# A two-layer decoder trunk with routed experts: the router's product taken ahead of the norm, the first expert weights asked for later, and the operand splits in another order

## The reference, cut to what matters

```python
for i in range(DEPTH):                       # DEPTH = 2, SEQ = 512, D_MODEL = 1024
    mix = swa_sink_attention(...) if i % 2 == 0 else forgetting_attention(...)
    x = layer_norm(ALPHA * x + mix, ln_gain[i, 0], ln_bias[i, 0])
    ffn = grouped_moe(x, w_router, b_router, w_gate[i], w_up[i], w_down[i])
    x = layer_norm(ALPHA * x + ffn, ln_gain[i, 1], ln_bias[i, 1])

def layer_norm(x, gain, bias):
    mu, var = mean(x), mean((x - mu) ** 2)
    return (x - mu) * rsqrt(var + 1e-5) * gain + bias

def grouped_moe(h, ...):                     # 16 experts in 4 groups of 4
    logits = h @ w_router + b_router         # (512, 16)
    # softmax; the best group by its two highest scores; in it the best two experts
    # act = silu(h @ w_gate[e]) * (h @ w_up[e]) * gate;  y = sum over e of act @ w_down[e]
```

## Time and profile before

| | |
|---|---|
| median of 3 runs | 919.23 us (918.41 to 920.52) |
| the profiled execution's own time | 919.96 us |
| its span | 918.2 us |
| TensorE busy | 888.0 us (97%) |
| VectorE busy | 552.9 us (60%) |
| ScalarE busy | 392.3 us (43%) |
| granted TensorE clock, mean | 0.996 |

### The profile page before, as it was taken

The page is one execution under the profiler, slowest core; times in us unless marked ns, Lnnn a source line. Parts: engine busy times, 40 slices in busy tenths (PEclk is TensorE's granted clock), DMA queues, the critical chain, the costliest instruction groups (busy, mean ns, idle before and its releaser), DMA issues.

```text
span 918.2 us, 12501 instructions
## 1 busy us (share of the span) xinstructions
PE 888.0 (97%) x4480; PEld 616.2 (67%) x4480; DVE 552.9 (60%) x1141; ACT 392.3 (43%) x787; POOL 120.1 (13%) x138
## 2 busy tenths in 40 slices
PE   8999999999999999989999999999999999999996
PEld 7887777884666665557878886655786565666553
DVE  4544786548766677773332223777456777677846
ACT  4322787001555655540132224777301355555540
POOL 2000232103010000120000000323111200000030
PEclk9999999999999999999999999999999999999999
DMA  9962000019999998644054222120106999999352
GB/s 347 302 253 92 2 1 1 24 47 351 350 382 389 379 389 322 222 180 163 21 184 138 92 93 92 46 71 24 69 24 241 312 380 382 374 384 406 124 197 96
DMA packets 49446, 182.36 MB, mean 199 GB/s; under 512 B 6496, under 2 KB 6496, under 8 KB 41200
## 3 DMA queue, kind: packets, MB, share of 16 engines
q1 hardware_dynamic: 35712, 132.34, 38.6%
q0 software_dynamic: 9392, 34.12, 11.3%
q10 hardware_dynamic: 4288, 15.21, 4.2%
HBM read 159.60 MB, written 22.05 MB: 198 GB/s over the span
## 4 chain that ended last, share of the span: by engine, by line
PE 89%; DVE 5%; DMA 3%; issue 2%; ACT 1%; SPq 1%; POOL 0%; DVEq 0%; ACTq 0%; POOLq 0%
PE bank L613 17%; PE bank L615 16%; PE bank L614 16%; PE bank L896 11%; PE bank L727 4%; PE bank L708 4%; PE bank L865 3%; PE bank L570 3%; PE bank L752 2%; PE bank L771 2%; PE bank L527 2%; DMA ring<-in_swa_w_in 2%; PE bank L813 2%; PE bank L541 1%; DMA ys<-arena 1%
## 5 line engine op out<-in xcount | busy, mean ns | idle before, releaser
L1492 DVE TENSOR_TENSOR gu_low<-ring,gu_high 128x1024 fp32r<-128x1024 f32 x128 | 151.2, 1221 | 46.9 <-ACT gu_high L1116 46.8
L1116 ACT CAST gu_high<-ring 128x1024 fp32r<-128x1024 f32 x128 | 127.6, 1048 | 18.5 <-DVE arena L1626 18.5
L896 PE MATMUL bank<-ring,arena 128*96 128x512 f32 x256 | 115.8, 595 | 2.0 <-issue 2.0
L613 PE MATMUL bank<-gu_high,rows_high 128*96 128x512 f32 x256 | 113.0, 442 | 2.5 <-DVE rows_low L1610 2.5
L614 PE MATMUL bank<-gu_low,rows_high 128*96 128x512 f32 x256 | 101.5, 397 | 0.0
L615 PE MATMUL bank<-gu_high,rows_low 128*96 128x512 f32 x256 | 101.1, 395 | 0.0
L896 PEld LDWEIGHTS bank<-ring,arena 128*96 128x96 f32 x256 | 39.7, 164 | 55.0 <-issue 54.0
L1048 ACT ACTIVATE arena<-arena,nmax 128x256 f32<-128x256 f32 (+3 forms) x128 | 66.8, 523 | 20.9 <-DVE nmax L1385 10.8
L471 POOL TENSOR_TENSOR low<-ring,high 128x512 fp32r<-128x512 f32 x32 | 40.7, 1272 | 220.5 <-ACT high L1076 220.5
L613 PE MATMUL bank<-high,x_high 128*128 128x512 f32 x160 | 64.2, 401 | 1.3 <-DVE low L1286 1.1
L615 PE MATMUL bank<-high,xlow 128*128 128x512 f32 x160 | 62.9, 393 | 0.0
(11 more groups left out here) (244 smaller groups left out, 1543.7 us busy)
## 6 DMA issues: line engine op xcount, KB each, us to landing
ring<-in_w_gate SPq DMA_DIRECT2D x32, 1024.0 KB, 12.3
ring<-in_w_up SPq DMA_DIRECT2D x32, 1024.0 KB, 15.0
ring<-in_w_down SPq DMA_DIRECT2D x32, 1024.0 KB, 14.9
ring<-in_fox_w_in SPq DMA_DIRECT2D x6, 2048.0 KB, 9.4
ys<-arena ACTq DMA_DIRECT2D x28, 384.0 KB, 7.7
ys<-lnp POOLq DMA_DIRECT2D x1, 4608.0 KB, 24.3
ring<-in_swa_w_in SPq DMA_DIRECT2D x2, 2048.0 KB, 17.2
ring<-in_swa_w_o SPq DMA_DIRECT2D x2, 2048.0 KB, 15.9
```

Source lines behind the costliest of these rows:

```text
L613: eng.matmul(out, ah, wh, start=(c == 0), stop=False)
L896: mm = eng.matmul(bank[5 + half][0:CAP, :], hT[:, b, c, :], w[:, c, half * BLK:(half + 1) * BLK], start=(c == 0), stop=(c == FC - 1))
L1116: eng.copy(gu_high[u % 2][:, :, part, :], slot_gate_up(use)[:, :, part, :]).then_inc(S("gu_high"), 1)
L1492: eng.tensor_tensor(gu_low[use % RING][:, :, part, :], slot_gate_up(use)[:, :, part, :], gu_high[u % 2][:, :, part, :], ALU.subtract).then ...
```

## The change

Four edits. First, the router's product is taken of the residual before the norm. With r the reciprocal root and mu the mean of a row, logits = r * (x @ (gain*wr - mean over rows of gain*wr)) + (bias @ wr + br). The adjusted weights and biases of both layers are made once, in the last four groups of layer 0's projection: four more small loads, a transpose and a product on PE, some twelve small operations on DVE. `turn_x` waits for `res_done` and no longer for `x_ready`; DVE copies the transposed tile first and applies the norm then (`turned_norm`); the routing has one more operation of 64 elements (rows times r).

Second, the third tile's router product stands inside the last group of the output projection, and the 16 dummy matmuls behind it are 3.

Third, SP asks for less before the routing. `down 0` is still asked for at the end of the output projection; gate and up 2, down 1, gate and up 3 and down 2 wait for the first expert's rows, down 3 for the second's.

Fourth, orders: expert 0's low parts are made in pairs at t = 1 and t = 2; six of the eight value-weight subtractions ahead of the mixed statistics go behind the first tile's norm; the banks are opened ahead of the hot rows' transposes; the rope load shares a semaphore with tile 1's load.

```diff
@@ SP
+                        for i in range(2 * DEPTH):
+                            vec = (ln_gain, ln_bias)[i % 2][i // 2, 0]
+                            eng.dma_start(ln_rows[KC * i:KC * i + KC, :], vec.rearrange("(c p) -> c p", p=P)).then_inc(S("const_in"), 16)
...
                 eng.wait_ge(S(f"wo_done{l}"), OUT_BLOCKS * NT)
-                for u in range(RING):
+                load_down(EXP_USE[l], l, 0, S(f"d_loaded{EXP_USE[l] % RING}"))
+                for u in range(1, RING):
+                    if u < RING - 1:
+                        eng.wait_ge(S(f"xe_in{l}0"), 16)
+                    else:
+                        eng.wait_ge(S(f"xe_in{l}1"), 16)
+                    if u + 1 < RING:
+                        k = EXP_USE[l] + u + 1
+                        load_gate_up(k, l, u + 1, S(f"w_loaded{k % RING}"))
                     k = EXP_USE[l] + u
-                    if u == RING - 1:
-                        eng.wait_ge(S(f"xe_in{l}1"), 16)
-                    if u >= OUT_BLOCKS:
-                        load_gate_up(k, l, u, S(f"w_loaded{k % RING}"))
                     load_down(k, l, u, S(f"d_loaded{k % RING}"))
@@ PE
+                elif a in ("00", "10"):
+                    eng.wait_ge(S("res_done"), 2 * (t + 1) + OUT_BLOCKS * NT * int(a[0]))
...
+                            if k == GROUPS[0] - 4:
+                                eng.wait_ge(S("const_in"), 144)
+                                eng.transpose(bank[7][:, 0:4 * KC], ln_rows[0:4 * KC, :], ident[0:4 * KC, 0:4 * KC]).then_inc(S("wr_pe"), 1)
+                            if k == GROUPS[0] - 3:
+                                eng.wait_ge(S("consts"), 1)
+                                eng.wait_ge(S("wr_dve"), 1)
+                                eng.matmul(bank[7][:, 0:4 * NE], ones, wr_sum, start=True, stop=True).then_inc(S("wr_pe"), 1)
+                    eng.wait_ge(S("wr_dve"), 2)
...
+                            if g == OUT_BLOCKS * NT - 1 and c == KC // 2:
+                                route(t - 1)
...
-                    if t >= 1:
+                    if 1 <= t < NT - 1:
                         route(t - 1)
-                hum(16)
+                hum(3)
                 turn_x(NT - 1, f"{l}0")
@@ ACT
                 for t in range(NT):
+                    evac_x(f"{l}0", t)
                     eng.wait_ge(S(f"x_ready{l}0"), t + 1)
                     eng.dma_start(xd[t * P:(t + 1) * P, :], xres[:, t, :]).then_inc(S("x_stored"), 16)
-                    evac_x(f"{l}0", t)
@@ DVE
+                def turned_norm(t):
+
+                    v = xres[:, t, :]
+                    evac_x_tile(f"{l}0", t)
...
+                    link(eng.scalar_tensor_tensor(v, v, mv[:, t, 0:1], lnp[:, 0, :], ALU.subtract, ALU.mult))
+                    eng.wait_ge(S(f"rstd{l}0"), t + 1)
+                    eng.scalar_tensor_tensor(v, v, rstd[:, t:t + 1], lnp[:, 1, :], ALU.mult, ALU.add).then_inc(S(f"x_ready{l}0"), 1)
...
-                link(eng.tensor_tensor(lg, lps, tiles(br[:, :]), ALU.add))
+                link(eng.tensor_tensor(lg, lps, over(rstd[:, :], NE), ALU.mult))
+                link(eng.tensor_tensor(lg, lg, tiles(bl[:, l, :]), ALU.add))
...
-                    value_weights_low(KC, 2 * KC)
+                    value_weights_low(KC, KC + 2)
...
                                 state_low(t - 1)
+                                if t == 1:
+                                    value_weights_low(KC + 2, 2 * KC)
```

More of the change, by code:

```diff
@@ L532, in turn_x @@
                 if a == "in":
-                    eng.wait_ge(S(f"x_in{t}"), 16)
+                    eng.wait_ge(S(f"x_in{t}"), 32 if t == 1 else 16)
+                elif a in ("00", "10"):
+                    eng.wait_ge(S("res_done"), 2 * (t + 1) + OUT_BLOCKS * NT * int(a[0]))
                 else:
@@ L1311, in _ @@
                         j, t = k // NT, k % NT
-                        if k == GROUPS[0] - 1:
-                            eng.wait_ge(S("const_in"), 80)
+                        if k == GROUPS[0] - 3:
+                            eng.wait_ge(S("wr_pe"), 1)
+                            link(eng.tensor_copy(ln_cols, bank[7][:, 0:4 * KC]))
+                            for i in range(2 * DEPTH):
+                                ins = eng.tensor_tensor(wr_ln[:, :, i, :], wr_in,
+                                                        ln_cols[:, KC * i:KC * i + KC].unsqueeze(2).to_broadcast([P, KC, NE]), ALU.mult)
+                            link(ins)
+                            eng.tensor_reduce(wr_sum, wr_ln.rearrange("p c j n -> p (j n) c"), X, ALU.add).then_inc(S("wr_dve"), 1)
+                        if k == GROUPS[0] - 1:
+                            eng.wait_ge(S("wr_pe"), 2)
+                            for m in range(DEPTH):
+                                col = 2 * m * NE
+                                link(eng.tensor_scalar(ln_cols[:, 0:NE], bank[7][:, col:col + NE], 1.0 / D, None, ALU.mult))
+                                link(eng.tensor_tensor(wr[:, m, :, :], wr_ln[:, :, 2 * m, :],
+                                                       ln_cols[:, 0:NE].unsqueeze(1).to_broadcast([P, KC, NE]), ALU.subtract))
+                                ins = eng.tensor_tensor(bl[:, m, :], bank[7][:, col + NE:col + 2 * NE], br[:, :], ALU.add)
+                            ins.then_inc(S("wr_dve"), 1)
+                            eng.wait_ge(S("const_in"), 144)
                             link(eng.tensor_scalar(sink[:, :], sink[:, :], -1.0, None, ALU.mult))
```

45 lines of the change are left out of this document (26 added, 19 removed).

## The result

The changed kernel takes 927.77 us (median, 923.71 to 930.65), the kernel before on the same chip 918.98 us. The ratio is 1.0088, with a 95% interval of 1.0066 to 1.0110: slower by 0.9%, where 0.3% was forecast. The profiled execution took 927.08 us (span 925.3) against 919.96, so 7.1 us are to be found between the two traces. In the experiments the same instructions stand a few lines away again (L886 or L890, for instance, are the transposes of an expert's rows).

What follows compares the result with a forecast made beforehand. TensorE is 97% busy, partly with dummies, waiting through routing; expert-phase transfers are nearly as full. Terms +1.7 + 1.6 - 1.6 + 0.4 = +2.1 gave 922.1 profiled, 921.3 as median, taken as 922.0 us; range 914.3 to 925.8.

Steps and rivals of the forecast that it cites:

- Part 1: Routing in each layer: with the router's product ahead of the norm, routing starts earlier, gain 1.8 us a layer.
- rival (d): Routing: the norm stays on the path because another wait ends last, the tile's store to `xd` starting 2 us later; no chance given.
- Part 4: Expert phase: held loads make expert 4's up weight late, TensorE waits 3.5 us; net 1.7 slower in layer 0, 1.6 in layer 1.
- Part 2: Between the layers: six subtractions leave the path to the first normalised tile, TensorE's 1.60 us wait goes, gain 1.6 us.
- Part 3: Projection: one added transpose, one product and two semaphore waits, loss 0.4 us, bounds 0.2 and 1.0.
- Rival (c): Clock falls behind TensorE's waits, each adding 1.7 us: 923 to 925; chance 0.12 for falls in both layers or the dummies.
- The sum: Whole kernel: +1.7 + 1.6 - 1.6 + 0.4 = +2.1 us, profiled execution 922.1.
- Rival (a): Expert phase: the weights come in time, nine transfers landing within 31.0 us; 914.4 us, chance 0.18.

Runs made afterwards that it cites:

- Experiment 1: Changed kernel with the old order of SP's loads (expert 2's three weights and down 1 asked for as the output projection ends): 928.9 us, ratio 1.0092.
- experiment 8: experiment 3's kernel with DVE's low parts of the value weights back in one piece ahead of the first norm: 919.01 us, ratio 0.9989.
- experiment 12: experiment 3's kernel with the router's weights and biases placed behind the big scratch tile; one execution, product groups 5.97 us apart, 6.03 in the changed kernel.
- experiment 5: Changed kernel (full hold) with the gathers of experts 2 and later held until gate and up 2 have landed; one execution: 929.3 us.
- Experiment 3: Changed kernel with gate and up 2 asked for at once behind down 0, the other five loads still held: 917.2 us, ratio 0.9971.
- experiment 9: Changed kernel (full hold) with 22 and 14 dummy products in TensorE's wait for expert 2's weights in layers 0 and 1: 929.78 us, ratio 1.0097.
- full hold: The changed kernel's own order of loads, seven of them asked for only behind the first or second expert's rows: 927.77 us, ratio 1.0088.
- experiment 10: experiment 3's order of loads with the down weight of expert 3 moved behind gate and up 4: 916.66 us, ratio 0.9960.
- experiment 13: experiment 10's kernel with the tile placement of experiment 12: 916.5 us, ratio 0.9966.
- experiment 7: The kernel before with experiment 3's order of loads: 921.75 us, ratio 1.0022.
- experiment 2: The kernel before with the held loads alone, nothing else of the change: 932.19 us, ratio 1.0135.
- experiment 6: Changed kernel with gate and up 2 and down 1 asked for once all four normalised tiles are stored, other loads held: 928.05 us, ratio 1.0079.
- experiment 4: Changed kernel with the five loads behind gate and up 2 held until the second rows: 927.57 us, ratio 1.0082.
- experiment 11: experiment 10's kernel with GpSimd's two loads of the next norm's rows moved behind the eighth gather: 921.37 us, ratio 1.0015.

## Why the prediction was wrong

The direction was right and the time was 5.8 us too low, outside the range.

**Part 1, router ahead of the norm: right, with a blind spot.** Forecast -1.8 us a layer, measured -1.93 and -1.88, with the waits in the forecast order (copy of xT, two norm operations, routing). But rival (d), the store to `xd`, was given "nothing of its own", as four transfers had left the queue ahead of it. With the hold this was so (2.9 us). Experiment 1 shows what it hides: with the old order of loads the same move costs far more than it gives. Measured against the gains of the other parts (-1.93 - 1.88 - 1.75 + 0.86 = -4.7), its 8.9 us above the kernel before mean 13.6 us lost, in the main to late rows (the traces give 7.3 us in layer 0 and 5.6 in layer 1). The hold was no separate loss, as the prediction's Part 4 had it, but stood in place of that one.

**Part 2, between the layers: right.** Forecast -1.6, measured -1.75 in the ledger; experiment 8, which takes it back, is 1.8 us slower, with the wait of 1.77 us back in its trace.

**Part 3, projection: under-sized.** Forecast 0.4, measured 0.86, inside its bounds of 0.2 and 1.0. The two groups with the new operations take 6.40 and 6.25 us against 6.02 of their neighbours: 0.61 for a transpose and a product that were priced at 0.23 or so. The rest is the slower rhythm of all groups (0.05 us in each, some 0.4 us in eight; experiment 12), which no step of the forecast could contain, less some 0.15 us that comes back behind them.

**Part 4, the held weights: the failed step.** Its price was 3.5 and 3.4 us for a late up 4. The start of the experts lost 6.86 and 4.34. Two things in the step were wrong.

The first is the size of up 4's delay. Nine transfers were given 34.5 us; in layer 0 they took 37.3 (226.28 to 235.91 + 27.7), and up 4 landed at 263.6, not at 260.2. The step took the stretch behind 230.06 as its model, "with about as many gathers and stores between". But at 226 four gathers are in flight or about to start, and in the model fewer are. In layer 1 the nine took 35.2 us, forecast 36.1.

The second is "Expert 2's pair may be late as well, but its wait is not added, since up 4's landing sets the time". In the traces up 2's landing came to be felt first (TensorE's waits of 5.33 and 3.47 us), and up 4 was just in time for what that left. Up 2 was never reckoned. The trace before had a 1 MB transfer in second place that landed 10.0 us after its issue (the one issued at 230.43). Set at 226.65 that ends at 236.7, and up 2 was wanted at 236.9 (its landing at 242.2 less the wait of 5.33), so "may be late" rested on no slack at all. And it took 15.5, because of the gathers; experiment 5 takes them away and gets 7.3.

How the loss divides can be estimated. Experiment 3's third down product starts 5.0 us after the late up 4 lands (260.2 to 265.2). On that measure up 4 alone would have put this product at 268.5 in layer 0, against 262.1 without any wait (222.04 + 40.1, the distance in the kernel before): 6.4 us. In layer 1 the same sum gives 2.7 us. So the mechanism of the prediction is good for some 9.1 of the 11.2 us lost, where it was priced at 6.9, and the pair that it set aside and the clock for the other 2. Experiments 5 and 9 bear this out: with up 2 early, or the clock held, the third down product of layer 0 waits for up 4 and starts as late as with the full hold, within 0.4 us (though in experiment 5 the late rows of expert 2 had already cost 4 us by the second). The division stays an estimate, since up 4's landing itself depends on what TensorE's delay does to the other transfers.

**Rival (c), the clock: right in kind.** Both waits are followed by a fall, worth 1.6 us in layer 0 (5.17 - 3.6) and 2.5 in layer 1 (6.14 - 3.6), where 1.7 was named. Less of it counts than that: in layer 1 the old fall of the earlier trace rows did not come this time, and experiment 9 shows that in layer 0 up 4 would have taken most of it.

**The sum.** Forecast +2.1: -1.8 - 1.8 - 1.6 + 0.4 + 3.5 + 3.4. Measured: -1.93 - 1.88 - 1.75 + 0.86 + 6.86 + 4.34 = +6.5, of 7.1 in the device time of the two profiled executions. The 4.3 us by which Part 4 was too small are nearly all of the miss between these (5.0, since 922.1 was forecast for the profiled execution). Rival (a), weights in time, had 914.4; experiments 10 and 13, where they nearly are, give 916.7 and 916.5. Their profiled executions hold a fall of the clock of some 1.7 us that comes long ahead of these loads (last section); less that, experiment 10's 917.4 would be 915.7.

## What to carry to other kernels

When loads are moved behind an event, reckon the landing of each in turn against the moment at which it is wanted, the first one first, and with the other queues' traffic of that very stretch; a wait at the first hides those of all the others. When work is moved off one path, follow its result to every reader: here the norm left the router's path and came to stand in front of a store that gates the next gather, and that had been slow all along (10.0 us) without being felt. And an urgent small transfer (a store of 2.9 us, a gather of 4.2) is worth an emptied queue, but only what is really urgent should be held: of the seven loads that the changed kernel asks for only behind the rows, letting two go at once made 0.9% slower into 0.3% faster.

## What was not expected of the hardware

A gather of 384 KB goes from 4.2 to 8.1 us, and a store of 512 KB from 2.9 to 9.3 or 10.0, when 3 to 5 MB of weights had been asked for some 5 us earlier on another engine's queue. The store's first packet then moves 3.7 us after its issue and not 0.8. A 1 MB weight goes from 7.3 to 15.5 us beside the gathers; the transfer engines are then busy to 1.0 while they move 250 to 296 GB/s.

The rhythm of the fp32 products in the projection changes by 1% (6.02 to 5.97 us for 24 products and four transposes, in every group) with where the operands lie in SBUF: 640 bytes higher is slow, the old place and 512 bytes lower are not. Which of the operands and what rule of addresses does it was not tried.

Whether the clock falls behind a short wait differs from profile to profile, with nothing in the instructions there to tell why. At the end of layer 0's attention TensorE waits 0.84 us for DVE in every kernel. The two windows behind it, in the changed kernel and in experiment 10:

```profile
154.00:157.00 3.00, 2.16 (x14) 1.81 (x14) 1.14 (x3) 1.00 (x2) 1.10 (x1) 1.00 0.00 0
157.00:160.00 3.00, 3.00 (x15) 2.43 (x14) 0.31 (x1) 3.00 (x4) 0.00 (x0) 1.00 0.00 0
```

```profile
154.00:157.00 3.00, 2.16 (x11) 1.83 (x11) 0.73 (x3) 0.65 (x2) 1.05 (x1) 0.73 0.00 0
157.00:160.00 3.00, 3.00 (x11) 2.38 (x10) 0.66 (x1) 3.00 (x4) 0.00 (x0) 0.71 0.00 0
```

Granted 1.00 throughout in the one, 0.73 and 0.71 in the other, which costs 0.27 x 3 + 0.29 x 3 = 1.7 us. Of 16 profiles, 9 have this fall and 7 don't (experiment 7, with the old program there, has it too; the kernel before and experiment 2 don't). The same holds for the wait of 1.23 us ahead of the first expert product: where the rows are in time (all but experiments 1 and 6) it is followed by a fall 7 times in 28, in layer 1 before, in layer 0 of experiments 4, 11 and 12, in both of experiment 8 and in layer 1 of experiment 9. So a part of the scatter of 4 to 8 us between runs of one kernel is likely this, and a ledger of two profiles should be read for such windows first.
